# The end of a two-block network by halves of its tokens, squares summed on VectorE, and the modulation sums in groups of 32 columns

## The reference

```
def rms_norm(x, gain): y = x * rsqrt(mean(x*x, axis=-1) + EPS); return y * gain
# first block
h = h + hgrn2_mixer(rms_norm(h, attn_norm[0]));  h = h + conv_ffn(rms_norm(h, ffn_norm[0]))
h = h + dsa_mixer(rms_norm(h, attn_norm[1]));    h = h + conv_ffn(rms_norm(h, ffn_norm[1]))
x = rms_norm(h, final_norm)
# second block
for i in range(2):
    mod = silu(c) @ ada_w[i] + ada_b[i]          # 1024 -> 6 * 1024
    sh1, sc1, g1, sh2, sc2, g2 = split(mod, 6)
    h = rmsnorm(x, norm1_g[i]) * (1 + sc1) + sh1
    x = x + g1 * mixer(h)                        # attention, then hyena
    h = rmsnorm(x, norm2_g[i]) * (1 + sc2) + sh2
    x = x + g2 * conv_ffn_2(h)                   # 1024 -> 2 * 2816 -> 1024
return rmsnorm(x, final_g)
```

## Time and profile before

| what | value |
|---|---|
| time, median of 3 runs | 2891.96 us (2889.69 to 2896.49) |
| profiled execution, its own time | 2890.2 us |
| its span, first to last instruction | 2888.4 us |
| mean granted TensorE clock | 0.985 of 2.4 GHz |
| PE busy | 2773.1 us, 96% |
| DVE, ACT, POOL busy | 60%, 36%, 3% |
| chain that ended last, by engine | PE 86%, DVE 7%, ACT 2%, transfers 2% |

### The profile page before, as it was taken

The page is one execution under the profiler, slowest core; times in us unless marked ns, Lnnn a source line. Parts: engine busy times, 40 slices in busy tenths (PEclk is TensorE's granted clock), DMA queues, the critical chain, the costliest instruction groups (busy, mean ns, idle before and its releaser), DMA issues.

```text
span 2888.4 us, 35842 instructions
## 1 busy us (share of the span) xinstructions
PE 2773.1 (96%) x14656; PEld 2250.6 (78%) x14656; DVE 1728.3 (60%) x2488; ACT 1028.3 (36%) x1495; POOL 90.1 (3%) x156
## 2 busy tenths in 40 slices
PE   7999799999998999999999999999999999999998
PEld 6778688888875588888776688888888787888886
DVE  4287657475668557575556647564665888553443
ACT  3244434242333534242434633232332222432322
POOL 0000000000001300000001400000000000000000
PEclk9999999999999999999999999999999999999999
DMA  6711024443232124343321025454432110333221
GB/s 162 158 44 44 30 89 149 126 143 108 73 97 81 30 85 153 124 141 111 88 82 44 1 65 193 159 178 138 143 100 70 34 33 26 107 104 100 88 92 41
DMA packets 261803, 276.85 MB, mean 96 GB/s; under 512 B 23496, under 2 KB 230856, under 8 KB 261641
## 3 DMA queue, kind: packets, MB, share of 16 engines
q1 hardware_dynamic: 231448, 219.51, 25.0%
q10 hardware_dynamic: 30192, 55.05, 5.9%
HBM read 267.19 MB, written 7.34 MB: 95 GB/s over the span
## 4 chain that ended last, share of the span: by engine, by line
PE 86%; DVE 7%; ACT 2%; DMA 2%; issue 1%; SPq 1%; ACTq 0%; POOL 0%; DVEq 0%
PE ps L554 23%; PE ps L556 23%; PE ps L555 23%; PE ps L1154 3%; PE ps L790 2%; PE ps L1186 2%; PE ps L918 1%; DMA sb<-in_hgrn_w_in 1%; PE ps L1113 1%; PE ps L935 1%; PE ps L612 1%; DVE sb L1826 1%; PE ps L1132 1%; DVE sb L2192 1%; PE ps L952 1%
## 5 line engine op out<-in xcount | busy, mean ns | idle before, releaser
L554 PE MATMUL ps<-sb 128*128 128x512 f32 (+2 forms) x3448 | 1286.7, 373 | 31.6 <-ACT sb L1388 5.5
L556 PE MATMUL ps<-sb 128*128 128x512 f32 (+2 forms) x3448 | 1268.0, 368 | 0.0
L555 PE MATMUL ps<-sb 128*128 128x512 f32 (+2 forms) x3448 | 1267.9, 368 | 0.0
L554 PEld LDWEIGHTS ps<-sb 128*128 128x128 f32 x3448 | 651.2, 189 | 162.0 <-issue 36.0
L556 PEld LDWEIGHTS ps<-sb 128*128 128x128 f32 x3448 | 650.7, 189 | 112.4
L555 PEld LDWEIGHTS ps<-sb 128*128 128x128 f32 x3448 | 651.3, 189 | 108.9 <-issue 1.2
L1826 DVE TENSOR_TENSOR sb<-sb 128x2048 fp32r<-128x2048 f32 (+2 forms) x196 | 438.4, 2237 | 357.8 <-ACT sb L1287 357.8
L1287 ACT ACTIVATE sb<-sb 128x2048 fp32r<-128x2048 f32 (+2 forms) x196 | 365.0, 1862 | 286.1 <-PE ps L556 266.7
L2062 DVE SCALAR_TENSOR_TENSOR sb<-ps,sb 128x511 f32<-128x511 f32 (+1 forms) x264 | 197.5, 748 | 172.2 <-ACT sb L1511 166.7
L1511 ACT ACTIVATE sb<-ps,sb 128x512 f32<-128x512 f32 x132 | 99.7, 772 | 233.7 <-PE ps L556 233.6
L2082 DVE SCALAR_TENSOR_TENSOR sb<-sb 128x512 f32<-128x512 f32 x168 | 126.0, 750 | 12.9 <-DVE sb L2082 0.5
(11 more groups left out here) (226 smaller groups left out, 2170.8 us busy)
## 6 DMA issues: line engine op xcount, KB each, us to landing
sb<-in_ffn_w_up SPq DMA_DIRECT2D x88, 1024.0 KB, 5.1
sb<-in_ada_w ACTq DMA_DIRECT2D x192, 256.0 KB, 3.2
sb<-in_ffn_w_down SPq DMA_DIRECT2D x32, 1024.0 KB, 5.0
sb<-in_ffn_w_down SPq DMA_DIRECT2D x16, 768.0 KB, 4.4
sb<-in_hy_w_in SPq DMA_DIRECT2D x12, 1024.0 KB, 5.1
sb<-in_hgrn_w_in SPq DMA_DIRECT2D x8, 1024.0 KB, 11.5
sb<-in_hgrn_w_in SPq DMA_DIRECT2D x16, 512.0 KB, 5.5
sb<-in_dsa_w_in SPq DMA_DIRECT2D x6, 1024.0 KB, 5.2
```

What stands on the lines that cost most here:

```text
L554: pe.matmul(o, al, bh, start=f, stop=False, **kw)
L555: pe.matmul(o, ah, bl, start=False, stop=False, **kw)
L556: m = pe.matmul(o, ah, bh, start=False, stop=l, **kw)
```

## The change

Four edits.

**Squares.** DVE adds the squares of tiles 1 to 5 onto those of tile 0 in SBUF (`accumulate`, tensor_tensor 128 x 512), and PE sums the total once: `squared(None)`, between column 0 and column 1 of item 3, waits for the accumulation of tile 5. Tiles 6 and 7 are summed as before. All of tiles 1 to 6 are squared into one buffer, so each square waits for the accumulation of the one before.

**Start by halves.** In `halved_start` half 0 of both items runs together, row tile by row tile; the banks of both are waited for at the start.

**Modulation.** PE sums a block with four products whose weights are a 128 x 32 matrix of ones and whose moving operand is the accumulator; DVE turns the result (transpose of 32 x 32 blocks) and adds the bias (`ada_end`), 24 times instead of three single adds.

**End.** The norm of r = 17 is taken by tokens on the partitions (squares as weights, one column of ones), tiles times gain go to `xg` on DVE without the norm's factor, the 32 transposes lie between the products of item 3, and ACT and DVE scale by the factor as they copy out of PSUM. Stores are eight of 256 KB instead of four of 512 KB.

```diff
+            def last_end(sem, key, banks, ready, tile):
+                kt = items[key]["kt"]
+                for j in range(2):
+                    b = banks[1][j]
+                    wait_bank(b)
+                    project_half(key, j, 0, b, range(kt), ready, tile).then_inc(*mark(sem, ("res", LAST, 6 + j, 0)))
+                    freed[b] = [("x", LAST, 6 + j, 0)]
+                    if j == 0:
+                        wait_bank(STAT)
+                        pe.wait_ge(*at("acc", LAST, 0, 5))
+                        token_sums(sq[1], True, False, range(4)).then_inc(*mark("pe_stat", ("sq_used", LAST, 0, None)))
+                    turned(j, 0)
+                for j in range(2):
+                    b, part = banks[0][j], (kt - 2, kt // 2)[j]
+                    wait_bank(b)
+                    project_half(key, j, 1, b, range(part), ready, tile)
+                    if j == 0:
+                        token_squares(0, 6)
+                        token_squares(0, 7)
+                    else:
+                        turned(0, 1)
+                        turned(1, 1)
+                    project_half(key, j, 1, b, range(part, kt), ready, tile).then_inc(
+                        *mark(sem, ("res", LAST, 6 + j, 1), *([("used", key)] if j else [])))
+                pe.wait_ge(*at("rms", "final2", 0))
+                token_squares(1, 6)
+                turned(2, 0)
+                turned(3, 0)
+                token_squares(1, 7)
+                turned(2, 1)
+                turned(3, 1)
...
                 stage, i = NEXT[r]
-                for half in range(2):
-                    ready = lambda k: [("h", stage, half, k, "hi"), ("h", stage, half, k, "lo")]
+                ready = lambda half, k: [("h", stage, half, k, "hi"), ("h", stage, half, k, "lo")]
+                for n in range(2):
+                    for b in banks[n]:
+                        wait_bank(b)
+                for k in range(NT):
                     for n in range(2):
-                        if half == 0:
-                            for b in banks[n]:
-                                wait_bank(b)
-                        for k in range(NT):
-                            for j in range(2):
-                                m = project_half(keys[n], j, half, banks[n][j], (k,), ready)
-                                if half and k == NT - 1:
-                                    m.then_inc(*mark(sem, done[n][j], *([("used", keys[n])] if j else [])))
-                                    freed[banks[n][j]] = then[n][j]
-                            if half == 0 and n == 0 and k == 2:
-                                squared_half(r, 1)
-                        if half == 0 and n == 0:
-                            spread_half(stage, i, 1)
+                        for j in range(2):
+                            project_half(keys[n], j, 0, banks[n][j], (k,), lambda k: ready(0, k))
+                    if k == 2:
+                        squared_half(r, 1)
+                    elif k == 5:
+                        spread_half(stage, i, 1)
+                for n in range(2):
+                    for k in range(NT):
+                        for j in range(2):
+                            m = project_half(keys[n], j, 1, banks[n][j], (k,), lambda k: ready(1, k))
+                            if k == NT - 1:
+                                m.then_inc(*mark(sem, done[n][j], *([("used", keys[n])] if j else [])))
+                                freed[banks[n][j]] = then[n][j]
...
                 def squared(j):
                     for i in ((0, 1) if gain else (0,)):
-                        if j == 0:
+                        if j is None:
                             wait_bank((STAT, OTHER)[i])
-                        pe.wait_ge(*at("sq", r, i, j))
-                        sums((STAT, OTHER)[i], (ht if i else sq)[j % 2], j == 0, j == NT - 1).then_inc(
+                            pe.wait_ge(*at("acc", r, i, 5))
+                        else:
+                            pe.wait_ge(*at("sq", r, i, j))
+                        sums((STAT, OTHER)[i], (ht if i else sq)[1 if j in (None, 7) else 0], j is None, j == NT - 1).then_inc(
                             *mark("pe_stat", ("sq_used", r, i, j), *([("stat", r, i)] if j == NT - 1 else [])))
...
-                        squared(4)
-                        squared(5)
+                        squared(None)
...
-                        if stats and n:
-                            squared(2 * n - 2)
-                            squared(2 * n - 1)
...
+                    blocks = ADA[n][2]
                     for b in range(done[0], upto):
-                        wait_bank(6)
+                        if b == 0:
+                            wait_bank(6)
+                        elif b < blocks - 1:
+                            pe.wait_ge(*at("ada_turned", n, b - 1))
                         pe.wait_ge(*at("ada", n, 8 * b + 7))
-                        for i in range(4):
-                            c = 4 * b + i
-                            m = pe.matmul(ps[6][:, c:c + 1], acc[b % 2][:, 128 * i:128 * i + 128], ones[:, 0:1], start=True, stop=True,
-                                          skip_group_check=True)
+                        own = acc[b % 2].rearrange("p (c g i) -> p g c i", g=4, i=32)
+                        for g in range(4):
+                            m = pe.matmul(ada_sums(n, b)[32 * g:32 * g + 32, :].rearrange("p (c i) -> p c i", i=32), ones[:, 0:32], own[:, g],
+                                          start=True, stop=True, skip_group_check=True)
...
+                    dst = (ht if i else sq)[1 if j in (0, 7) else 0]
+                    if j == 7:
+                        act.wait_ge(*at("sq_used", r, i, None))
+                    elif j >= 2:
+                        act.wait_ge(*at("acc", r, i, j - 1))
...
+            def accumulate(r, j, gain):
+                for i in ((0, 1) if gain else (0,)):
+                    one, total = ht if i else sq
+                    dve.wait_ge(*at("sq", r, i, j))
+                    if j > 1:
+                        dve.wait_ge(*at("acc", r, i, j - 1))
+                    dve.tensor_tensor(total[:, :], total[:, :], one[:, :], ADD).then_inc(*mark("dve_acc", ("acc", r, i, j)))
...
+            def gained(j, hs, name):
+                dve.wait_ge(*at("x", *((LAST, j) if len(name) == 2 else (LAST, *name[1:]))))
+                dve.tensor_scalar(xg[:, j, hs], x[:, j, hs], v("final2", j), 32.0, MUL, MUL).then_inc(*mark("dve_x", name))
+            def last_end():
+                for half in range(2):
+                    for j in (6, 7):
+                        if half and j == 7:
+                            rows(0)
+                            rows(1)
+                        added(LAST, j, half)
+                        gained(j, HALVES[half], ("xg", j, half))
+                    inverse(root[:, 2 * half:2 * half + 2], ("final2", half))
...
+                        if stats and 2 <= j < 6:
+                            accumulate(r, j - 1, gain)
+                        if r == LAST:
+                            gained(j, slice(0, L), ("xg", j))
                     if n < 3 or not stats:
                         ahead(keys[n])
+                    if stats and n == 2:
+                        accumulate(r, 5, gain)
+                    if late and n == 2:
+                        late()
...
+                def ada_end(b):
+                    layer, b0, blocks = ADA[n]
+                    c0, t = 48 * layer + 4 * (b0 + b), acc[b % 2][:, 0:128]
+                    dve.wait_ge(*at("ada_sum", n, max(b, blocks - 1) if b >= blocks - 2 else b))
+                    dve.transpose(t, ada_sums(n, b)).then_inc(*mark("dve_ada", ("ada_turned", n, b)))
+                    dve.wait_ge(*at("ada_turned", n, b))
+                    dve.tensor_tensor(mod[:, c0:c0 + 4], t.rearrange("p (c i) -> p c i", i=32)[:, :, 0], v("ada_b", c0, 4), ADD).then_inc(
+                        *mark("dve_ada", ("mod", n, b)))
...
+                for part in range(2):
+                    c = 512 * part
+                    sp.wait_ge(*at("out", tt, part))
+                    sp.dma_start(out[0, 128 * tt:128 * tt + 128, c:c + 512], ot[:, tt, c:c + 512]).then_inc(*mark("st_out", ("stored", tt, part), by=16))
```

More of the change, by code:

```diff
@@ L665, in halved_end, with token_sums, token_squares @@
                     freed[b] = [("x", r, 6 + j, 1)]
+            def token_sums(squares, first, last, of):
+                for tt in of:
+                    m = pe.matmul(ps[STAT][:, tt:tt + 1], squares[:, 128 * tt:128 * tt + 128], ones[:, 0:1], start=first and tt == 0, stop=last,
+                                  skip_group_check=True)
+                return m
+            def token_squares(half, j):
+                pe.wait_ge(*at("sq", LAST, 0, j, half))
+                token_sums(sq[j - 6], False, j == NT - 1, (2 * half, 2 * half + 1)).then_inc(
```

(13 more changed lines are left out.)

104 lines of the change are left out of this document (48 added, 56 removed).

## The result

The changed kernel takes 2924.35 us (median of 4 runs, 2921.36 to 2925.96), against 2893.07 for the kernel before beside it (4 runs): ratio 1.0107, 95% interval 1.0089 to 1.0124, so 31.3 us slower. The forecast was 2909, from 2894 to 2921. The direction is right and the time lies outside the range. The profiled span is 2923.9 us; before it was 2888.4, so the two profiled executions lie 35.5 us apart, 4 more than the medians.

What follows compares the result with a forecast made beforehand. PE, busy 96% of the span, was taken as the bound. The terms +20.6 + 7.5 - 1.8 + 1 - 2 - 7.7 gave +17.6 us on the profiled 2890.2, forecast as a median of 2909 us, range 2894 to 2921.

Steps and rivals of the forecast that it cites:

- steps 1 to 4: Six residuals with their starts: sums saved, PE waits for the accumulation, clock falls, starts reordered; +26.3 us together.
- step 5: Residual r = 8: two groups of 16 sums go, a wait of some 4 us comes; +1 us (-1 to +4).
- step 6: Modulation: grouped sums save 3.0 us on 21 blocks, waiting for DVE's turn costs 1 in ffn2; -2 us (-3 to +3).
- step 7: End of the program: 21.5 us against 28.4 after item 2 of r = 17, plus 0.8 saved sums; -7.7 us (-5 to -10).
- step 3: PE's clock falls to half pace behind the six new waits, 1.4 us lost each; +7.5 us (0 to +12).
- Step 2: Six residuals: PE waits 4.8 us (kt = 8) for tile 5's accumulation behind DVE's low part; +20.6 us net of saved sums.
- Steps 1, 2 and 4: Six residuals without the clock: two sum groups saved (0.77 us each), waits for the accumulation, net +20.6; reordered starts -1.8.
- Step 4: Six starts by halves: nothing at the four ffn starts, -0.9 us at each of the two others; -1.8 us.
- rival D: The clock falls at the end too, slowing transposes and some 30 products: 2914 us, chance 0.06.
- rival B: Faster: the accumulation is ready when PE asks and no clock falls: 2868 us; chance 0.08, including all up to no change.
- C: Rival with more lost: four ffn starts find banks held, 2 us each, and r = 8 costs 4: 2920 us, chance 0.15.

Runs made afterwards that it cites:

- e1: Kernel before with only the squares part (DVE accumulates tiles 0 to 5, PE sums once), in eight residuals including the last: 2925.64 us, ratio 1.0114.
- e2: Kernel before with only the new order of the six starts by halves: 2892.17 us, ratio 0.9998.
- e3: Kernel before with only the modulation part, four grouped sums per block turned on DVE: 2895.17 us, ratio 1.0005.
- e4: Kernel before with only the new end of the last residual, its squares accumulated on DVE there alone: 2884.59 us, ratio 0.9970.
- e7: Kernel after with 30 added products of 256 columns ahead of PE's wait for the accumulation in six residuals: 2910.15 us, ratio 1.0056.
- e5: Kernel after with DVE's accumulation of tile 5 moved ahead of the weight item's low part: 2881.49 us, ratio 0.9961.
- e11: Kernel before with only the squares part, tile 5 accumulated ahead of the low part: 2883.30 us, ratio 0.9976.
- e9: Kernel after with tile 5 accumulated ahead of the low part and DVE's modulation turn one slot sooner: 2875.48 us, ratio 0.9943.
- e12: Kernel of e9 with half 1's sums behind the second shared row instead of the third, its spread behind the fourth instead of the sixth: 2867.26 us, ratio 0.9916.
- e8: Kernel before with only the grouped modulation sums, DVE's turn of a block one slot sooner: 2881.84 us, ratio 0.9968.

## Why the prediction was right in its direction and wrong in its size

Forecast and traces, product by product against the trace before, in us. A residual is taken from the last product of its item 1 to the third item of the next stage; the modulation is what ffn0, ffn1 and ffn2 gain or lose between two residuals; the end starts behind item 1 of r = 17. Each figure is of one pair of executions, and places where nothing was changed differ by up to 2 us in them, the first 373 us by more.

| place | forecast | kernel after | part alone |
|---|---|---|---|
| six residuals with their starts (steps 1 to 4) | +26.3 | +33.4 | e1 +30.1, e2 -1.0 |
| r = 8 (step 5) | +1 | +4.2 | e1 +2.6 |
| modulation (step 6) | -2 | +2.5 | e3 -0.9 |
| end (step 7) | -7.7 | -6.4 | e4 -7.9 |
| everywhere else | 0 | +1.8 | |
| sum | +17.6 | +35.5 | |

**The step that failed is step 3, the clock.** It was given 7.5 us and had six places; the clock cost 14.1 us at these six (e7) and also fell where the step had no term: behind the wait of r = 8 (2.3 us), behind two waits of the modulation (some 3) and at the end (1.5). Together that is some 13 of the 17.9 us between the forecast's sum and the traces. The mechanism, waits that end in a slow clock, was right; the size of this term was not.

- **Step 2 held** to a tenth at r = 14: a wait of 4.8 us was worked out, 4.89 came; from the end of item 2 the accumulation was due 7.6 us later, and 7.77 after 2519.72 it ended. Six waits of the six residuals sum to 29.3 us (33.2 less 3.93 at r = 8), the forecast's six to some 30. The two with kt = 6 were forecast at 5.5 and came at 4.98 and 5.04. The cause, a low part that waits for ACT in front of the accumulation, is shown by e5: take it away and 42.9 us go.
- **Step 3 was mis-sized**: the duration came from one row, where 3.34 us at half pace followed a wait of 3.86. Here the clock stayed at 1.2 GHz for 6.8 us at r = 1, 4, 10 and 14, and for 3.4 at r = 5 and 13. At r = 14 some 26 products were slow, not 16: 5.5 us of half pace is 2.4 lost. The bound of 12 was too low as well. The length is not the wait's alone: behind the same wait of 4.80 us at r = 10 it is 6.8 us in the kernel after and 3.4 in e1. What decides between the two stays open.
- **Steps 1, 2 and 4 together** gave +18.8; the six residuals lose 33.4 us between the two profiles, 19.3 without the clock's 14.1. They held. The sums that go were forecast at 11 us with r = 8; e11 has 7.8 there in its trace, net of the waits that stay.
- **Step 4 held alone**: nothing at the four ffn starts and -0.9 at each of the two others was forecast, and e2's trace has +0.8 in the four and -0.8 and -0.9 at the two; the medians can't tell it. In the mended kernel (e9) the new order loses 4 to 6 us, and there the step's two opposite mechanisms, the sums of half 1 that come late and the waits in half 0 that go, no longer balance: e12 moves the sums up and gets the gain without the loss.
- **Step 5**: +1 within -1 to +4; the profiles have +4.2, just over the upper end. The wait of 3.93 us was forecast (4). The sums that go gave back 1.2 us each time, and the clock, 6.8 us at 0.50 behind the wait, took 2.3; the step had no term for it.
- **Step 6 had both of its terms wrong**, -2 forecast. A group of four sums costs 0.56 us and not the 0.75 taken over from the group of eight, so the saving was 7.5 us (e8) and not 3. And PE's wait for DVE's turn, given 1 us at one stage, was 6.4 at three in e3 and 6.8 in the kernel after. In e3's trace the two leave -0.9, since the errors cancel in part; in the kernel after the clock fell behind two of the waits, and it is +2.5. The text had named DVE's order (one slot after the block) and didn't look at what stands in that slot. It is the low part again, the very obstacle of step 2.
- **Step 7 held**: -7.7 forecast, -7.9 measured (e4). The accumulation came 4.0 us after item 2, 3.9 had been worked out. The last copy ends 17.6 us after item 2 in e4, forecast 17.5, and 19.3 in the kernel after, where the clock fell for 3.4 us behind the wait of 1.80: a part of rival D came too. From the last copy to the end of the span it is 3.7 us, 4.0 had been given. The eight stores of 256 KB landed 2.7 us after issue (median, 2.1 to 3.5), the four of 512 KB before also 2.7 (2.6 to 3.1), against estimates of 2.6 and 3.2: halving them brought no earlier landing. The transposes (L694 alone, a stretch of the end: us, PE, PEld, PEclk, DMA share, GB/s) ran at full clock between products:
```profile
2914.40:2918.70 4.30, 2.76 (x22) 2.57 (x23) 1.00 0.46 171
```
  They took 0.125 us each, near the 0.11 of the earlier trace rows. The Trainium skill's rule of transposes at the low clock (TensorE: Matmul & The Clock Gate, Part 4: PE-mode transpose) is not borne out here either, though with products between them these transposes test it less than those of the earlier trace rows.

Small slips of the prediction that move nothing: 2907.8 + 1.8 is 2909.6; the idle time before 2502.32 is 0.82 in the row, not 0.98; with the clock rival B needs 2.9 us less wait a place, not 3.1.

The medians, alone against forecast: squares +33.2 for +29.1 (steps 1 to 3 and 5), starts -0.3 for -1.8, modulation +2.7 for -2, end -7.9 for -7.7. They carry the chance of where else the clock fell: 3.9 of e1's and 6.4 of e3's lag were there before the first residual. Of the rivals C, the case of more lost, came nearest with 2920, by r = 8, where it had +4; but its other term, the starts, was not what filled the gap. The upper end of the range, 2921, lies 12 us over the forecast; the upper bounds of steps 2, 3, 5 and 6 alone add up to 15.5.

## What to carry to other kernels

An instruction that another engine waits for must not stand, in its own engine's order, behind one that waits for a third engine: look in the timeline for the long "idle before" just ahead of it, and put the short one into that idle time. When a change adds such a wait at one place, check every other new wait of the change for the same neighbour. A wait of 5 us on the engine that bounds costs 5 and the slow clock behind it, here half as much again: give the clock a term at every new wait, not only at the longest. Moving the question later on the waiting engine or the answer earlier on the other is worth nearly the same. And before a difference of a few us is read as a part's worth, compare the traces at a product ahead of the first edit.

## What the runs showed of the hardware

- The granted clock fell to 0.50 behind every wait of 4.7 us and more at the sums, but for either 3.4 or 6.8 us: in the kernel after, waits of 4.80 us (r = 10) and 5.04 us (r = 13) had 6.8 and 3.4, and the 4.80 of r = 10 had 3.4 in e1.
- 30 products in place of 3.7 of the 4.9 us of idleness kept the clock at 1.00 (e7).
- The fall is not tied to long waits alone, and one length of wait can have it or not: waits of 1.80 (end), 2.42 (r = 13) and 3.21 us (modulation) had it behind them in the kernel after, while those of 1.79 (end, e7) and 2.88 (modulation, e3) had not; at r = 13 one of 2.05 in e2 had not and one of 2.06 in e9 had. Those of 0.89 to 1.21 us at the sums of r = 14 in e5 and e7 had not.
- The six waits of 1.10 us between 188 and 325 us (L782 in before), the same in every kernel, had a low clock behind one of them in before, two in the kernel after, four in e3 and none in e9. So one execution differs from another: of the 25 of the kernel before beside e1 to e4, the two longest (2898.0 and 2896.7 us) had a mean granted clock of 0.981, the three shortest (2887.6 to 2888.0) 0.983 to 0.985.
- Four sums with 32 columns of weights cost 0.56 us in the stream, eight 0.77: halving the number of products saves a quarter of the cost.
